# Modulation sums along rows, a residual shared by two engines, and a compression placed among dense units

## The reference, cut to what matters

```python
cs = jax.nn.silu(c)                                     # c: (1, 1024)
sh_m, sc_m, g_m, sh_f, sc_f, g_f = jnp.split(cs @ mod_w[i] + mod_b[i], 6, axis=-1)
...
shift, scale = jnp.split(cs @ kv_mod_w + kv_mod_b, 2, axis=-1)
...
x = x + g_m[:, None, :] * rmsnorm(y, norm_post_mix[i])
h = adaln(x, norm_pre_ffn[i], sh_f, sc_f)
x = x + g_f[:, None, :] * rmsnorm(swiglu(h, ffn_w_in[i], ffn_w_out[i]), norm_post_ffn[i])
...
def compress(t, pe, w1, w2):
    blk = t[:, idx] + pe[None, None, :, None, :]
    blk = jnp.moveaxis(blk, 3, 2).reshape(bsz, n_cmp, NSA_KV_HEADS, CMP_BLOCK * NSA_HEAD_DIM)
    return jax.nn.silu(blk @ w1) @ w2
```

## Time and profile before

| | us |
|---|---|
| median of 3 runs | 2997.19 |
| lowest, highest | 2997.13, 3005.85 |
| profiled execution, its own time | 2998.98 |
| its span | 2997.0 |
| PE busy | 2688.0 (90%) |
| DVE busy | 1237.9 (41%) |
| ACT busy | 1052.5 (35%) |
| POOL busy | 894.7 (30%) |

### The profile page before, as it was taken

The page is one execution under the profiler, slowest core; times in us unless marked ns, Lnnn a source line. Parts: engine busy times, 40 slices in busy tenths (PEclk is TensorE's granted clock), DMA queues, the critical chain, the costliest instruction groups (busy, mean ns, idle before and its releaser), DMA issues.

```text
span 2997.0 us, 36121 instructions
## 1 busy us (share of the span) xinstructions
PE 2688.0 (90%) x12652; PEld 2089.6 (70%) x12652; DVE 1237.9 (41%) x2059; ACT 1052.5 (35%) x1526; POOL 894.7 (30%) x379
## 2 busy tenths in 40 slices
PE   4888859799999899999899998999878999899997
PEld 3666637578887586666688885689646787687785
DVE  7699952555553613654411115564111211431122
ACT  3245443332222413555432224732322233342231
POOL 1223214234434210001244442301202444244442
PEclk8999979899999888999999999999978999999998
DMA  5344412245554210001122231200101333122221
GB/s 226 109 146 166 154 52 92 78 168 182 183 177 141 81 67 22 15 15 50 57 98 98 85 105 63 78 29 29 56 0 50 105 106 106 57 99 92 98 98 49
DMA packets 65674, 275.69 MB, mean 92 GB/s; under 512 B 7296, under 2 KB 7552, under 8 KB 57760
## 3 DMA queue, kind: packets, MB, share of 16 engines
q1 hardware_dynamic: 54576, 202.18, 20.3%
q10 hardware_dynamic: 10992, 72.03, 6.8%
HBM read 272.02 MB, written 2.16 MB: 91 GB/s over the span
## 4 chain that ended last, share of the span: by engine, by line
PE 71%; DVE 15%; issue 5%; ACT 5%; DMA 2%; DVEq 1%; POOL 0%; ACTq 0%; POOLq 0%
PE STAT_G L273 27%; PE G L273 26%; DVE mod_acc L334 3%; PE B L273 1%; DMA mod_w<-in_modw 1%; PE B L1574 1%; DVE tn L1810 1%; PE B L867 1%; DVE x L491 1%; DVE y L490 1%; PE STAT_G L378 1%; PE B L738 1%; PE NRM L904 1%; PE STAT_G L885 1%; DVE mod_first L314 1%
## 5 line engine op out<-in xcount | busy, mean ns | idle before, releaser
L262 POOL TENSOR_TENSOR w_lo<-raw,w_hi 128x1024 fp32r<-128x1024 f32 x375 | 894.5, 2396 | 2061.2 <-ACT w_hi L254 2061.1
L254 ACT ACTIVATE w_hi<-raw 128x1024 fp32r<-128x1024 f32 x375 | 385.7, 1052 | 463.8 <-PE G L273 172.7
L273 PE MATMUL STAT_G<-h_hi,w_hi 128*128 128x512 f32 x928 | 373.6, 403 | 16.1 <-DVE tn L1810 6.2
L273 PE MATMUL G<-h_hi,w_hi 128*128 128x512 f32 x944 | 373.5, 396 | 6.4 <-DVE yc_lo L443 2.2
L273 PE MATMUL G<-h_hi,w_lo 128*128 128x512 f32 x944 | 367.6, 389 | 0.0
L273 PE MATMUL G<-h_lo,w_hi 128*128 128x512 f32 x944 | 367.5, 389 | 0.0
L273 PE MATMUL STAT_G<-h_lo,w_hi 128*128 128x512 f32 x928 | 364.8, 393 | 0.0
L273 PE MATMUL STAT_G<-h_hi,w_lo 128*128 128x512 f32 x928 | 364.5, 393 | 0.0
L273 PEld LDWEIGHTS STAT_G<-h_hi,w_hi 128*128 128x128 f32 x928 | 176.5, 190 | 57.6 <-issue 16.1
L273 PEld LDWEIGHTS G<-h_hi,w_hi 128*128 128x128 f32 x944 | 177.2, 188 | 49.2 <-issue 6.1
L273 PEld LDWEIGHTS G<-h_lo,w_hi 128*128 128x128 f32 x944 | 177.2, 188 | 37.7 <-issue 1.9
(11 more groups left out here) (424 smaller groups left out, 3760.7 us busy)
## 6 DMA issues: line engine op xcount, KB each, us to landing
raw<-in_units SPq DMA_DIRECT2D x375, 512.0 KB, 3.4
mod_w<-in_modw ACTq DMA_DIRECT2D x48, 1024.0 KB, 4.8
mod_first<-in_modw ACTq DMA_DIRECT2D x8, 1024.0 KB, 21.9
acsb<-acs ACTq DMA_DIRECT2D x16, 512.0 KB, 3.6
cw<-in_cw ACTq DMA_DIRECT2D x2, 2048.0 KB, 7.6
x<-in_x SPq DMA_DIRECT2D x1, 2048.0 KB, 11.9
out<-x SPq DMA_DIRECT2D x1, 2048.0 KB, 6.2
const<-in_const SPq DMA_DIRECT2D x1, 1084.0 KB, 16.5
```

Source lines behind the costliest of these rows:

```text
L254: act.activation(w_hi[s][:, :], raw[s][:, :], ACT.Identity).then_inc(hi_done, 1)
L262: pool.tensor_tensor(w_lo[s][:, :], raw[s][:, :], w_hi[s][:, :].bitcast(F32), ALU.subtract).then_inc(lo_done, 1)
L273: ins = pe.matmul(out[0:m, :], a[s][:, k * P:k * P + m], b[:, c], start=(n == 0 and q == 0), stop=(n == len(blocks) - 1 and q == 2))
```

## The change

Three parts.

**Modulation sums by rows.** The weights are packed so that an output is a partition and the 1024 inputs lie along the row, two half rows of 1024 for each group. The row `silu(c)`, copied to all partitions by a DMA, takes the place of the 8 columns. A sum is two instructions of 1024 columns that multiply a half row with it and add up along the row into a column of `mod`. The chain of 8, the matmuls against ones and the PSUM columns are gone. The row lies in the columns of `const` that hold the mask and the levels; these are loaded at the end of ffn0. In ffn0 the sum now stands behind the tile's own DVE work.

**Residual.** DVE scales all 8 blocks and then adds blocks 4 to 7; POOL adds blocks 0 to 3, behind the splits of the two units that open the next stage.

**Keys and values.** The keys' compression stands behind unit 5, its second layer behind unit 7, the values' compression behind unit 10 and its second layer behind the first query unit. The position products become sums over 16 blocks of `cw1` on DVE (`positions`), in two halves each, and one matmul against ones for each half of the columns. The query's h is formed block by block with the units. The keys' half of `cw1` is asked for before the statistics of the stage.

```diff
-        def mod_sum(v, link, g, i=0):
+        def mod_row_sums(v, src, g):
+
+            for b in range(2):
+                half_row = src[:, b * D:(b + 1) * D]
+                ins = v.scalar_tensor_tensor(half_row, half_row, 1.0, silc, ALU.mult, ALU.mult,
+                                             accum_out=mod[:, bass.ds(g * 2 + b, 1)] if not isinstance(g, int)
+                                             else mod[:, 2 * g + b:2 * g + b + 1])
+            ins.then_inc(mod_used, 1)
...
+        def mod_sum(v, g, i=0):
             g = i + g
-            src = mod_w[:, :]
             v.wait_ge(mod_ready, g * 16 - 112)
-            v.wait_ge(mod_reduced, g)
-            link(v.tensor_scalar(mod_acc[:, :], src[:, 0:MODW], csil[:, 0:1], None, ALU.mult))
...
+            mod_row_sums(v, mod_w, g)
...
             for i in range(KC):
                 c = slice(i * T, (i + 1) * T)
-                link(v.scalar_tensor_tensor(y[:, c], y[:, c], amul[:, i:i + 1], NRM[:, :], ALU.mult, ALU.mult))
+                v.scalar_tensor_tensor(y[:, c], y[:, c], amul[:, i:i + 1], NRM[:, :], ALU.mult, ALU.mult).then_inc(ys_done, 1)
+            for i in range(KC // 2, KC):
+                c = slice(i * T, (i + 1) * T)
+                v.wait_ge(ys_done, KC * posts[name] + i + 1)
                 v.tensor_tensor(x[:, c], x[:, c], y[:, c], ALU.add).then_inc(x_done, 1)
...
+        def residual_pool(pool, name):
+
+            for i in range(KC // 2):
+                c = slice(i * T, (i + 1) * T)
+                pool.wait_ge(ys_done, KC * posts[name] + i + 1)
+                pool.tensor_tensor(x[:, c], x[:, c], y[:, c], ALU.add).then_inc(xp_done, 1)
...
+            for t in range(4, 12):
+                for i in query_blocks(t):
+                    h_vector_scaled(v, k0, i)
+                    h_vector_low(v, k0, modcol(64), h1_hi, h1_lo, i)
+                if t >= 5:
+                    consume(t - 1)
+                if t == 8:
+                    v.wait_ge(kvc_mm, 1)
+                    v.tensor_copy(kcmp[:, :], B7[:, 64:64 + 2 * NCMP]).then_inc(kvc_done, 1)
+                    positions(v, link, 1, 0)
+                if t == 9:
+                    positions(v, link, 1, 1)
...
+            for m in range(8 * part, 8 * part + 8):
+                p, w = col(("pe_k", "pe_v")[c], m), cw1[:, m * 256:(m + 1) * 256]
+                if m == 0:
+                    ins = v.tensor_scalar(pos[c], w, p, None, ALU.mult)
+                else:
+                    ins = v.scalar_tensor_tensor(pos[c], w, p, pos[c], ALU.mult, ALU.add)
```

More of the change, by code:

```diff
@@ L338, in mod_sum @@
-            ins.then_inc(mod_used, 1)
-        def mod_reduce(pe, g, i=0):
-            g = i + g
-            pe.wait_ge(mod_used, g + 1)
-            for b in range(2):
-                ins = pe.matmul(modp[:, bass.ds(g * 2 + b, 1)] if not isinstance(g, int) else modp[:, 2 * g + b:2 * g + b + 1],
-                                mod_acc[:, b * P:(b + 1) * P], ones1, start=True, stop=True)
-            ins.then_inc(mod_reduced, 1)
+            mod_row_sums(v, mod_w, g)
         def mod_bias(v, g0, n, count):
-            v.wait_ge(mod_reduced, count)
+            v.wait_ge(mod_used, count)
@@ L608, in ffn_vector @@
                     body = SLOTS // per
-                    with loop(v, n // body, link, 7 * body if mods is not None else 0) as i:
+                    with loop(v, n // body, None, 0) as i:
                         for j in range(body):
-                            if mods is not None:
-                                mod_sum(v, link, m0 + j, i * body)
                             k = k0 + hidden + j
@@ new lines, in compress @@
+        def compress(pe, c):
+            pe.wait_ge(w1_ready, 16 * (c + 1))
+            pe.wait_ge(t2_a, 2 * c + 2)
+            pe.wait_ge(t2_v, 2 * c + 2)
+            if c:
+                pe.wait_ge(hid_done, 2)
+                pe.wait_ge(kvc_done, 1)
+            view = (t2k, t2v)[c][:, :].rearrange("p (h t) -> p h t", h=4)
+            for hh in range(2):
+                for m in range(16):
+                    w = cw1[:, m * 256 + hh * P:m * 256 + (hh + 1) * P]
+                    pe.matmul(B6[:, hh * 124:(hh + 1) * 124].rearrange("p (h n) -> p h n", h=4), w,
+                              view[:, :, 2 * m:2 * m + 16 * (NCMP - 1) + 1:16], start=(m == 0), stop=(m == 15))
+            pe.wait_ge(pos_done, c + 1)
+            for hh in range(2):
+                ins = pe.matmul(B7[:, hh:hh + 1], pos[c][:, hh * P:(hh + 1) * P], ones1, start=True, stop=True)
+            ins.then_inc(cmp_mm, 1)
@@ L768, in nsa_load, with first_compress_load, hidden, query_blocks @@
         def nsa_load(act):
+            act.wait_ge(mod_used, 56)
+            act.dma_start(const[:, LATER], dram["const"][:, LATER]).then_inc(later_loaded, 16)
             for name, dst in (("rope", rope), ("cw2", cw2)):
                 act.dma_start(dst[:, :], dram[name]).then_inc(att_in, 16)
+        def first_compress_load(act):
+            act.dma_start(cw1[:, :], dram["cw1"][0:P, :]).then_inc(w1_ready, 16)
+        def hidden(act, link, c):
+            act.wait_ge(cmp_mm, c + 1)
+            if c == 0:
+                act.dma_start(cw1[:, :], dram["cw1"][P:2 * P, :]).then_inc(w1_ready, 16)
+            link(act.activation(hb[:, 0:2], B7[:, 0:2], ACT.Identity))
+            for hh in range(2):
+                act.activation(hid[:, (2 * c + hh) * 124:(2 * c + hh + 1) * 124], B6[:, hh * 124:(hh + 1) * 124],
+                               ACT.Silu, bias=hb[:, hh:hh + 1]).then_inc(hid_done, 1)
+        def query_blocks(t):
+            return {4: (0, 1), 11: ()}.get(t, (t - 3,))
         def nsa_kv_scalar(act, link):
-            act.dma_start(cw1[:, :], dram["cw1"][0:P, :]).then_inc(w1_ready, 16)
             k0 = splits["h_mix1"]
@@ L1997, in ssm_vector @@
             v.wait_ge(cb_done, 16)
-            with loop(v, 8, link, 2 * (7 + 3)) as i:
+            with loop(v, 8, link, 2 * 3) as i:
                 for j in range(2):
@@ L2075, in _ @@
             sp.dma_start(x[:, :].rearrange("p (k t) -> p k t", k=KC), dram["x"]).then_inc(x_loaded, 16)
[L2076 removed]
+            for part in (slice(0, LATER.start), slice(LATER.stop, NCONST)):
+                sp.dma_start(const[:, part], dram["const"][:, part]).then_inc(loaded, 16)
             for j in range(SLOTS):
@@ L2091, in _, with splits @@
         def _(pool):
-            for u in range(SLOTS):
-                split(pool, u)
-            with pool.Fori(0, NU // SLOTS - 1) as i:
-                for j in range(SLOTS):
-                    split(pool, SLOTS + j, i)
-            for u in range(NU // SLOTS * SLOTS, NU):
-                split(pool, u)
+            def splits(u0, u1):
+                for u in range(u0, SLOTS):
+                    split(pool, u)
+                u0 = max(u0, SLOTS)
+                n = (u1 - u0) // SLOTS
+                with pool.Fori(0, n) as i:
+                    for j in range(SLOTS):
+                        split(pool, u0 + j, i)
+                for u in range(u0 + n * SLOTS, u1):
+                    split(pool, u)
+            done = 0
+            for name, stage in (("post_mix0", "ffn0"), ("post_ffn0", "kv"), ("post_mix1", "ffn1"), ("post_ffn1", "gdn_ab"),
+                                ("post_mix2", "ffn2"), ("post_ffn2", None)):
+                ahead = at[stage] + 2 if stage else NU
+                splits(done, ahead)
+                residual_pool(pool, name)
+                done = ahead
         @block.scalar
```

210 lines of the change are left out of this document (104 added, 106 removed).

## The result

The median went from 2999.07 us (4 runs) to 2935.36 us (4 runs, 2934.99 to 2935.67); the ratio is 0.9779, 95% interval 0.9767 to 0.9792. That is 64 us less, where 112 were forecast, and outside the range. The direction was right, the size was not.

What follows compares the result with a forecast made beforehand. Dense matrix products on PE, 71% of the chain, were taken to bound the kernel; gains come only where PE waits or does other work. Terms -7.5 - 5 - 16.5 - 33 - 13 - 37 = -112 us gave 2886 us, range 2866 to 2920.

Steps and rivals of the forecast that it cites:

- The new sum: Modulation sum on DVE as two 1024-element instructions: 2.7 us, bounds 2.4 and 2.9, 1.2 us less than before.
- Rival (a): DVE's accumulating form runs at half rate, 4.9 us per sum; only residuals and keys/values gain: 2968 us, 10%.
- Rival (c): DVE and POOL lock: half-rate sums each also meet a POOL split, 7.3 us per sum: 3076 us, slower than before, 2%.
- rival (b): PE savings become waits: POOL's adds 2.4 us each, ACT's wait costs ffn0 10 us, a position half exposed: 2925 us, 6%.
- Start and B/C: Kernel start, DVE keeping up with loads: -7.5 us; B/C part of the SSM, shorter sum and no reduction: -5 us.
- Loop: SSM loop over 16 tiles: 1.1 us less in each of 15 periods, -16.5 us (-13 to -19).
- ffn0: Sums and reductions cost ffn0 34.5 us over ffn1; nearly all would go: -33 us (-25 to -34.5).
- ACT's wait: In ffn0 ACT's next load waits for the sum, with weight preps behind it; 1.5 us left for that.
- Rival (d): ffn0's difference from ffn1 is DMA, not DVE; ffn0 keeps 20 of its 34.5 us: 2906 us, inside the range.
- Residuals: Six residuals, adds shared by DVE and POOL: 2.0 us each for five, 2.9 at the last, -13 us (-17 to +8).
- Keys and values: Key/value stage: position products, second cw1 load, PE's wait and slow unit leave PE's path: -37 us (-28 to -42).

Runs made afterwards that it cites:

- the one with both addresses right: Changed kernel with amul's 8 columns (32 bytes) allocated ahead of x and 16 unused columns (64 bytes) ahead of sq: 2885.91 us.
- with the clock held up: Against the one with both addresses right, four extra PE products nobody reads behind five residuals' statistics and the eight sums following each: 2876.86 us.

## Why the prediction was wrong, point by point

- **The step that failed** stands in its first paragraph: "most of the span is dense matrix products, which this change leaves alone". It left the instructions alone and moved their operands. That costs 0.16 us for each unit wherever PE is the bound: 10.1 us in ffn1, 9.8 in ffn0, 15.2 in the third mixer, 8.9 in ffn2 (changed kernel against the one with both addresses right); with what the other stages add and give back, 49.5 us between the medians 2935.4 and 2885.9. No rival had it, so the range ended 15 us below the result. With the addresses put right the forecast of 2886 is met by 2885.9, and that closeness is luck: the residuals gave 8 us less than forecast and keys/values 2, and the loop (4.8), the start (2.5) and 1 to 2 us each in three other rows of the table gave it back.
- **The new sum**: 2.37 us against 2.7 taken, below the lower bound. Rival (a), that the accumulating form runs at half rate, has fallen: 1.22 us for 1024 elements. The sentence of the Trainium skill, Vector Engine (DVE) Microarchitecture Reference, "Points that are easy to get wrong", does not hold for this form and f32; the measurement decides. Rival (c) fell with it. Of rival (b), whose 2925 lies nearest to the result, nothing came: POOL's adds take 1.24 us, ffn0 with the addresses right is within 0.4 us of ffn1, and keys/values came out at -35 to -37.
- **Start and B/C**: -12.5 forecast, -12.9 measured, by luck. The bias add came at 42.49, not at 40.1, so the start gave 5.1 us and not 7.5: two instructions met POOL's splits and took 2.1 us more each, and I had counted on one. B/C gave 7.8 where 5 were forecast, and the two errors cancel.
- **Loop**: a period of 15.27 us against 15.4 forecast, and 15.12 with the addresses right. Mis-sized by 0.1 to 0.3 us, on the side of the shorter sum; with the addresses right the -21.3 lie beyond the term's bound of -19.
- **ffn0**: -34.1 with the addresses right, nearly the whole 34.5 that the earlier trace rows offered. The 1.5 us kept back for ACT's wait were not needed, and the place of the sum, on which the forecast spent a chain of six durations, is worth nothing. Rival (d), the DMA, has fallen.
- **Residuals**: -5.0 against -13. The mechanism on DVE and POOL was right to 0.1 us; the pace behind it was mis-sized. "The four last need about 0.93 us each" took PE's sums at full clock. It let them follow the last add of POOL, as if the first four were done by then. But PE comes to the sums after 4.4 us of idle, runs the first ones at 0.50, and needs 9.97 us for the eight, 8.53 with the clock held up. Then the residual is 12.9 us, near the 12.5 of the forecast. The earlier trace rows could not show it: they have the last sum alone, which ran at 1.00.
- **Keys and values**: -37 forecast, -37.1 measured and -35.2 with the addresses right. The term was right in sum. Its largest part was given as 21.3 us: where the compression now stands, the positions on PE cost 25.2 us of the stage, since they also lower the clock for the unit behind them. Where they stood before, other work stood behind them, and what they cost there was not run. What the other parts were worth singly was not measured.

## What to carry to other kernels

When a change adds, drops or resizes a buffer, compare the start addresses of the operands of the hot products before and after, and look at the start-to-start time of one product in a stage that the change does not touch: if it moved, the layout did it. Keep the operands of the products, stationary and moving, a multiple of 256 bytes apart (pad once, ahead of the group), at least for fp32r products like these. When a shorter chain ahead of PE brings nothing, read the granted clock in windows of a few us: PE's own work right behind an idle gap may have become the pace, and products that nobody reads, put into the gap, can hold the clock. And when a total lands on its forecast, compare it stage by stage before believing the terms.

## What the runs showed of the hardware that I had not expected

- A 128x512 fp32r product starts every 226.7 ns when its operands are a multiple of 256 bytes apart, and on average every 231 to 233.8 ns (a unit of 5.54 to 5.61 us over 24) where some distance leaves 32, 128, 192 or 224 by 256. At the low clock both take 426.7 ns. A distance 32 bytes off a multiple of 256 cost the kernel before 44 us (1.5%) and the changed one 50 us (1.7%).
- Putting one of two wrong addresses right gains nothing, since the distance is still wrong: 2935.19 and 2935.55 us, and only both together 2885.91.
- The accumulating scalar_tensor_tensor reads two f32 sources from SBUF at 1.2 ns per element with its fixed part, and its accumulator read is 0.08 us.
- PE's granted clock falls from 1.00 to 0.50 under 64 one-column products issued back to back, though PE counts as busy in each window. The products' starts lie 112 ns apart before and 213 ns after it has fallen.
- The same residual code took 12.9 us with PE kept busy ahead of it, and 13.5 to 14.9 us without: when in it the clock comes back differs (6 to 9 us after the first scaling of the second residual it is 0.58 in one trace and 0.71 in another).
